# Another order of the recurrence steps 4 to 7 in the gated delta rule: the independent products ahead of the dependent ones

## The reference

```
a_mat = beta * (k k^T) * d_strict
sol = triangular_solve(a_mat, [beta v, beta gam k])          # u0, w
p_intra = (q k^T) * d_incl;  q_g = q * gam;  k_d = k * exp(cum_end - cum)
def step(s, (w, u0, p, qg, kd, ge)):
    u = u0 - w s
    o = qg s + p u
    s = ge * s + kd^T u
    return s, o
```

## Time and profile before

| what | value |
|---|---|
| median of 3 runs | 3936.43 us (3927.51 to 3937.48) |
| the profiled execution | 3936.43 us |
| its span, first to last instruction | 3934.4 us |
| PE busy | 3618.2 us, 92% |
| DVE busy | 2245.2 us, 57% |
| ACT busy | 1249.9 us, 32% |
| POOL busy | 283.1 us, 7% |
| mean granted TensorE clock | 0.962 |
| second loop, layer 0 | 807.7 to 864.8 us |
| second loop, layer 1 | 2036.7 to 2093.6 us |

### The profile page before, as it was taken

How to read it: one execution, slowest core, us unless ns; L and a number is a source line. 1 busy time by engine, 2 the same in 40 slices (tenths; PEclk the granted TensorE clock), 3 DMA queues, 4 the chain that set the end, 5 groups by cost and what they waited for, 6 DMA issues and landing times. The chain is left out here.

```text
span 3934.4 us, 60111 instructions
## 1 busy us (share of the span) xinstructions
PE 3618.2 (92%) x24920; PEld 2241.2 (57%) x24920; DVE 2245.2 (57%) x3955; ACT 1249.9 (32%) x2191; POOL 283.1 (7%) x233
## 2 busy tenths in 40 slices
PE   7789988979989979897998999899999997999999
PEld 4367545765654457744775664466666665444443
DVE  3475357756653456456775666266666667433454
ACT  3253254434531234245423443112222222231001
POOL 0010000000000011010000000122222221000000
PEclk9899999989999989999998999999999998999999
DMA  4333212121032232311212004211111111312231
GB/s 155 99 87 96 81 43 76 55 82 42 13 134 108 97 97 82 120 32 52 65 58 106 11 27 152 67 33 44 44 44 39 43 33 44 119 52 83 89 108 47
DMA packets 301822, 281.14 MB, mean 71 GB/s; under 512 B 18016, under 2 KB 274144, under 8 KB 301552
## 3 DMA queue, kind: packets, MB, share of 16 engines
q1 hardware_dynamic: 301552, 277.30, 21.7%
HBM read 203.93 MB, written 73.33 MB: 70 GB/s over the span
## 5 line engine op out<-in xcount | busy, mean ns | idle before, releaser
L3386 DVE SCALAR_TENSOR_TENSOR cv<-glu,params,cv 128x1024 f32<-128x1024 f32 x240 | 361.0, 1504 | 6.4
L1471 PE MATMUL ps<-hT,w_cols 128*128 128x512 f32 x576 | 254.4, 601 | 13.6 <-PEq L158 13.6
L399 PE MATMUL ps<-hT,w_cols 128*128 128x512 f32 x448 | 204.7, 618 | 3.3 <-PEq L158 3.3
L1471 PEld LDWEIGHTS ps<-hT,w_cols 128*128 128x128 f32 x576 | 110.8, 193 | 152.3 <-issue 150.4
L3682 PE MATMUL ps<-hT,wr 128*128 128x512 f32 x360 | 161.7, 592 | 0.0
L399 PEld LDWEIGHTS ps<-hT,w_cols 128*128 128x128 f32 x448 | 88.4, 199 | 116.5 <-issue 116.5
L3362 POOL TENSOR_TENSOR Sp<-Sp,Rp 128x520 f32<-128x520 f32 (+1 forms) x56 | 88.6, 1582 | 565.2 <-DVE W L3403 565.2
L3145 PE MATMUL ps<-hT,w_f 128*128 128x347 f32 x384 | 117.2, 465 | 6.7 <-DMA w_f<-in_w_in 6.7
L3160 PE MATMUL ps<-w_i,hT 128*128 128x128 f32 x1024 | 120.7, 277 | 0.0
L3682 PEld LDWEIGHTS ps<-hT,wr 128*128 128x128 f32 x360 | 68.4, 190 | 86.1 <-issue 86.1
L3160 PEld LDWEIGHTS ps<-w_i,hT 128*128 128x128 f32 x1024 | 116.1, 192 | 2.2 <-issue 1.6
(11 more groups left out here) (929 smaller groups left out, 7307.8 us busy)
## 6 DMA issues: line engine op xcount, KB each, us to landing
w_cols<-in_w_in SPq DMA_DIRECT2D x32, 512.0 KB, 3.8
wr<-in_w_in SPq DMA_DIRECT2D x24, 512.0 KB, 5.1
hT_hbm<-hT SPq DMA_DIRECT2D x2, 4096.0 KB, 14.7
hT<-hT_hbm SPq DMA_DIRECT2D x2, 4096.0 KB, 14.5
fh<-hT_hbm SPq DMA_DIRECT2D x16, 512.0 KB, 4.5
fh_again<-hT_hbm SPq DMA_DIRECT2D x16, 512.0 KB, 4.7
x<-in_x SPq DMA_DIRECT2D x8, 512.0 KB, 8.6
ahead<-kb_hbm SPq DMA_DIRECT2D x16, 256.0 KB, 3.3
```

The source lines that it names most:

```text
L399: q = pe.matmul(ps[:, proj_bank(n, b), :], lhsT=wc[:, n % 3, k, :], rhs=hT[:, k, P + b * 512:P + (b + 1) * 512], start=(k == 0), stop=(k = ...
L1471: q = pe.matmul(ps[:, proj_bank(n, b), :], lhsT=wc[:, n % 3, k, :], rhs=hT[:, k, P + b * 512:P + (b + 1) * 512], start=(k == 0), stop=(k = ...
L3386: vec.scalar_tensor_tensor(out=cv[:, h % 2, :], in0=src, scalar=w, in1=cv[:, h % 2, :], op0=ALU.mult, op1=ALU.add).then_inc(*VEC(f"tap{h}_ ...
```

## The change

In the loop over s = 4 to 7, PE's and DVE's programs issue the same instructions in another order. The helper functions, the bank list `TURNS`, and ACT's, POOL's and SP's programs stay as they are. PE now issues `keys` and the first `pairs` ahead of `first_half`, the second `pairs` ahead of `across`, `out_of_state` ahead of `second_half`, and `values_in(s + 1)` ahead of `to_state`. DVE now does `decays(s + 1)`, `keys` and the first `query_pairs` ahead of `first_half`, and the second `query_pairs` ahead of `across`.

```diff
--- before.py
+++ after.py
@@ -1890,16 +1890,16 @@
                                 keys_on_state(s)
                                 if s < NT - 1:
                                     decays(s + 1)
+                                keys(s)
+                                pairs(s, 0, 0)
                                 first_half(s)
-                                keys(s)
+                                pairs(s, 1, 0)
                                 across(s)
-                                pairs(s, 0, 0)
+                                out_of_state(s)
                                 second_half(s)
-                                pairs(s, 1, 0)
-                                out_of_state(s)
-                                to_state(s)
                                 if s < NT - 1:
                                     values_in(s + 1)
+                                to_state(s)
                                 out_of_chunk(s)
 
                         @block.scalar
@@ -2188,14 +2188,14 @@
                             for s in range(4, NT):
                                 right_side(s)
                                 old_state(s)
-                                first_half(s)
-                                keys(s)
-                                across(s)
-                                query_pairs(s, 0)
-                                second_half(s)
-                                query_pairs(s, 1)
                                 if s < NT - 1:
                                     decays(s + 1)
+                                keys(s)
+                                query_pairs(s, 0)
+                                first_half(s)
+                                query_pairs(s, 1)
+                                across(s)
+                                second_half(s)
                                 new_state(s)
                                 if s == 4:
                                     rest_of_own(1)
```

## The result

The changed kernel takes 3976.45 us (median of 4; 3971.03 to 3991.58), the kernel before 3932.74 in the same runs. The ratio is 1.0117, with a 95% interval of 1.0086 to 1.0150. The forecast was 3951.4, a ratio of 1.004. The direction was right; the size was not.

A forecast was written before the change was run, and what follows sets the result against it. PE's own work, 14.58 us a middle step, was taken as the limit. New waits of 2.29 us in three middle steps plus 0.6 in step 7 gave 7.5 us a layer: 3936.4 + 15.0 = 3951.4 us, range 3936 to 3958.

The forecast's parts named there:

- The bound: Middle step: PE has 14.58 us of work in 14.58 us at full clock, so no order makes it less.
- The three waits: PE in a middle step: 0.26 us ahead of first `pairs`, 0.85 ahead of second, 1.18 ahead of `across`; 2.29 together.
- handover: DVE, between neighbouring operations: 0.08 us of overlap taken off each.
- the change of halves: DVE's copy L2078 reads partitions 64 to 127 after an instruction from 0: no overlap, +0.03 us.
- Step 7: Last step: wait of 0.93 us for `R` goes, 0.78 and 0.83 come; 13.32 us against 12.72, +0.6.
- The sum: Both layers: 3 x 2.29 + 0.6 = 7.5 us a layer, 15.0 us in all.
- Rival C: PE's clock falls behind gaps near 1 us, for 2 us of work a step: 12 us more, 3963; chance 0.03.
- the earlier loop: Evidence against the clock falling: same stage, PE busy 17.77 of 20 us with waits of this size, clock 1.00.
- Rival A: The chain's waits might already be part of the 14.58: 1.4 us faster, 3935; chance 0.07.
- its point of 7.2: If copy L2078 ended by 7.2 us into a step, `across` would not wait and the change would not be slower.
- Rival B: Waits come, but DVE's four operations run shorter or `gam` comes earlier: 3.3 us saved, 3948; chance 0.18.
- The range: Whole kernel: 3936 to 3958 us, from the not-slower case's end and the spread of the runs.

The follow-up runs named there:

- e6: Changed kernel plus useless products in both waits: 6 ahead of the second `pairs`, 2 ahead of `across`, in step 7 2 and 2; 3948.77 us, 1.0029.
- e9: Changed kernel plus 8 useless products behind `out_of_state`, on both array halves by turns, each half with its own PSUM bank; 3966.4 us, 1.0078.
- e5: Changed kernel plus 8 useless products on array rows 0 to 63 only, behind `out_of_state`, the waits left unfilled; 4008.99 us, 1.0179.
- e3: Kernel before, with only DVE's `decays(s + 1)` moved ahead of `first_half`, PE's order the old one; 3949.07 us, 1.0035.
- e1: Changed kernel plus useless products: 6 ahead of the second `pairs`, 7 ahead of `across`, in step 7 5 ahead of `across` and `to_state`; 3956.02 us, 1.0044.
- e7: Changed kernel plus 6 useless products ahead of the second `pairs` alone, none ahead of `across`; 3945.59 us, 1.0020.
- e12: Changed kernel plus 4 useless products ahead of `across`, the wait ahead of the second `pairs` left whole; 3943.96 us, 1.0022.

## Why the prediction was wrong

- **The bound (PE's own work, 14.58 us).** Right. No order shown here makes a middle step shorter.
- **The three waits, 0.26 + 0.85 + 1.18 = 2.29 us a middle step.** Right: 2.40 by the steps, 0.91 and 1.10 by their rows. From start to start, as the prediction counts, they are 0.16, 0.97 and 1.27. `across` starts with DVE's chain `gam`, L2067, L2061, L2052, L2078, as worked out. On DVE one handover was mis-sized: L2061 starts 0.02 after L2067 ends, where I took an overlap of 0.08. The one at the change of halves, L2078 behind L2052, is 0.04, where I took 0.03 and where the Trainium skill ("VectorE: DVE Perf Modes", "Two Vector instructions with no wait between them") says held; the trace agrees.
- **Step 7, +0.6.** Right in its size (13.43 against 12.72), and in its parts: the wait for `R` is gone, one ahead of `to_state` is new, 0.87 us in layer 0 and 0.8 in layer 1.
- **The sum, 15.0 us.** For what it held, right: e6, where the clock stays up, has loops 15.9 us longer. But it is a sum at full clock: it puts the clock's term at nothing. That is the step that failed. The runs show 25.7 us in its place, of the 41.6 that the loops grew by, and with the waits filled (e6) that term is gone and the 15.9 are left.
- **Rival C, the clock.** This is what happened, and I gave it 3 in 100 and 12 us. It was wrong in its chance and in its size. I priced 2 us of work a step, 16 in all, at 0.73 us more for each; the 58 us at the lower clock hold 32 us of work, at 0.80 more for each. The 0.73 was low because the fill's 4.54 us are at the lower clock for 3.4 us only. And the ground on which I set C aside was wrong: the earlier loop, busy 17.77 of 20 us at clock 1.00 with waits of 0.8 and 0.9, has much the same share of idle time, and still the two behaved differently. The trace of before had the other case too. In each of its four `join`s the clock falls for 3.4 us behind an idle time of 1.0 to 1.3 us, in the second one at 803.5, just behind

```profile
802.69 0.63 PE L1850 MATMUL ps<-RY,AT_g 32*32 32x32 f32 x28 [0.97 <-issue]
```

  The prediction took C's price from this place, but gave no weight to the fall coming in four of four, and let the earlier loop alone decide. How long the clock stays low depends on what stands behind the wait: e9 against e5 shows it, and e3 points the same way.
- **Rival A (not slower).** Did not happen; the copy ends at 8.51, past its point of 7.2.
- **Rival B (half of it).** No: DVE's four operations kept their length.
- **The Trainium skill.** The rule that I named beside rival C ("TensorE: Matmul & The Clock Gate", section "A second HAM failure mode: psum-queue depth-cycling") says that short idle times between groups of matmuls can make the clock go down and up. The traces agree, with three stretches at 0.50 in each of two executions behind waits of 0.9 and 1.1 us, and none where these were filled (e1, e6). I had let the earlier loop outweigh it.
- **The range** (3936 to 3958) held the waits and the spread of the runs and left out C; with 26 us for the clock it would have had to reach 3977.

Left open: why the clock falls behind some waits and not behind others of the same length, and why three times in eight steps. No run here varied the moment of a wait by itself. Open too is why e7 and e12 give up less time to the clock outside the loops than the kernel before.

## What to carry to other kernels

Where the matrix engine has work all the time, another order of that work gains nothing, and what it can cost is set by the engine that serves the chain: here the late copy on the vector engine, not the matmul. A wait of a microsecond in a stretch where the matrix engine was never idle cost nine more when the clock fell behind it, and what follows the wait changes how long the clock stays low; here it stayed low for 20 us behind a wait with no `pairs` after it and for 3.4 with them. Where a wait is left over, fill it with a measured length of useless products and look at the granted clock, and measure what one product takes first.

## What the runs showed of the hardware

A 64-row by 128-column float32 product on one half of the array takes 0.25 us in a row of such, and about 0.14 us by turns on both halves (0.0685 a record in `pairs`); at the lower clock the one-sided ones take 0.47. At the lower clock a block whose weights are 128 by 128 and whose moving part has 64 columns (`out_of_chunk`) goes from 2.89 to 5.38 us, 1.86 times as long, while PE's record shows it busy without a gap. A clock that has fallen need not show in PE's idle time: in the stretch from 816.28 to 837.03 PE is busy 20.75 of 20.75 us at 0.51.
